# Twelve 256-column projections of a two-layer trunk by seven quarter products instead of eight, the weight sums on GpSimd

## The reference, cut to what matters

```
for l in range(2):
    h = rmsnorm(x, attn_norm[l])                 # 256 tokens x 1024
    proj = h @ w_in[l]                           # 1024 x 3088: pa, pb, pc, pd side by side
    oa = rmsnorm(window_attention(rope(q, k), v, sinks))       # from pa: P11, P12
    ob = rmsnorm(gla_chunked(q, k, v, log_a)) * silu(g)        # from pb: P7, P8, P9/P10
    oc = rmsnorm(stick_breaking_attention(q, k, v))            # from pc: P4, P5, P6
    od = rwkv7_time_mix(pd, ...)                               # from pd: P0, P1, P2, P3
    x = x + concat(oa, ob, oc, od) @ w_out[l]
    h = rmsnorm(x, ffn_norm[l])
    x = x + (dense_swiglu(h) if l == 0 else top2_of_8_experts(h))
return rmsnorm(x, final_norm)
```

## Time and profile before

| | |
|---|---|
| Time, median of 3 runs | 960.59 us (960.5 to 961.04) |
| The profiled execution | 963.35 us, its span 961.4 us |
| PE busy | 945.6 us (98% of the span) |
| DVE, ACT, POOL busy | 379.5, 182.1, 146.7 us (39%, 19%, 15%) |
| Mean granted TensorE clock | 0.992 of full speed |
| Moved | 223.18 MB, mean 232 GB/s |

### The profile page before, as it was taken

How to read it: one execution, slowest core, us unless ns; L and a number is a source line. 1 busy time by engine, 2 the same in 40 slices (tenths; PEclk the granted TensorE clock), 3 DMA queues, 4 the chain that set the end, 5 groups by cost and what they waited for, 6 DMA issues and landing times.

```text
span 961.4 us, 28523 instructions
## 1 busy us (share of the span) xinstructions
PE 945.6 (98%) x12808; PEld 752.7 (78%) x12808; DVE 379.5 (39%) x811; ACT 182.1 (19%) x400; POOL 146.7 (15%) x164
## 2 busy tenths in 40 slices
PE   9999999999999999999999999999999999999996
PEld 8887875699999644788787659878878696969692
DVE  3415676476666555341566433122121213030204
ACT  3345241211111000224514121010000001010102
POOL 2000532033333421000063100000000000000000
PEclk9999999999999999999999999999999999999998
DMA  9843201545555545344310696999999999999931
GB/s 318 268 132 132 89 2 45 161 137 171 170 169 173 212 177 174 127 134 134 130 62 3 211 410 245 400 348 403 396 399 399 401 388 412 387 413 386 400 123 44
DMA packets 90114, 223.18 MB, mean 232 GB/s; under 512 B 6080, under 2 KB 53952, under 8 KB 89920
## 3 DMA queue, kind: packets, MB, share of 16 engines
q1 hardware_dynamic: 86528, 212.29, 59.6%
q0 software_dynamic: 1680, 5.90, 2.5%
q10 hardware_dynamic: 1840, 4.00, 1.3%
HBM read 215.89 MB, written 6.29 MB: 231 GB/s over the span
## 4 chain that ended last, share of the span: by engine, by line
PE 97%; ACT 2%; DVE 1%; issue 1%; POOL 0%; DVEq 0%; POOLq 0%; ACTq 0%
PE bank L629 94%; PE bank L640 1%; PE bank L1265 1%; ACT arena L1554 0%; PE bank L1008 0%; ACT hT L1409 0%; ACT arena L1551 0%; ACT arena L1414 0%; PE bank L976 0%; DVE arena L2036 0%; PE bank L779 0%; DVE hT L1855 0%; PE bank L803 0%; DVE arena L1804 0%; ACT arena L1527 0%
## 5 line engine op out<-in xcount | busy, mean ns | idle before, releaser
L629 PE MATMUL bank<-arena 128*64 128x96 f32 (+6 forms) x8592 | 504.9, 276 | 3.6 <-issue 1.4
L629 PEld LDWEIGHTS bank<-arena 128*64 128x64 f32 (+4 forms) x8592 | 381.3, 137 | 125.8 <-issue 103.9
L629 PE MATMUL bank<-hT,arena 128*64 128x128 f32 (+2 forms) x1548 | 164.5, 307 | 1.5 <-ACT hT L1409 0.9
L629 PEld LDWEIGHTS bank<-hT,arena 128*64 128x64 f32 (+2 forms) x1548 | 145.6, 152 | 16.4 <-issue 4.4
L1804 DVE TENSOR_TENSOR arena<-arena 128x512 f32<-128x512 f32 (+3 forms) x139 | 125.0, 913 | 51.2 <-ACT arena L1414 26.3
L629 PE MATMUL bank<-arena,hT 128*128 128x256 f32 (+3 forms) x556 | 135.1, 404 | 0.2
L629 PEld LDWEIGHTS bank<-arena,hT 128*128 128x128 f32 (+2 forms) x556 | 88.9, 181 | 36.4 <-issue 26.5
L1804 DVE TENSOR_TENSOR arena<-arena,bank 128x128 f32<-128x128 f32 (+3 forms) x135 | 48.9, 391 | 131.9 <-ACT arena L1617 104.5
L629 PE MATMUL bank<-tok,arena 128*64 128x128 f32 x1408 | 81.0, 273 | 0.0
L629 PEld LDWEIGHTS bank<-tok,arena 128*64 128x64 f32 x1408 | 78.2, 137 | 0.0
L1414 ACT COPY arena<-bank 128x512 f32<-128x512 f32 (+2 forms) x63 | 31.0, 496 | 173.3 <-PE bank L629 171.1
(11 more groups left out here) (207 smaller groups left out, 537.0 us busy)
## 6 DMA issues: line engine op xcount, KB each, us to landing
arena<-in_moe_w SPq DMA_DIRECT2D x128, 704.0 KB, 11.1
arena<-in_moe_w SPq DMA_DIRECT2D x40, 1024.0 KB, 8.8
arena<-in_ffn_w SPq DMA_DIRECT2D x33, 1024.0 KB, 5.6
arena<-in_w_in SPq DMA_DIRECT2D x22, 1024.0 KB, 5.3
arena<-in_w_out SPq DMA_DIRECT2D x8, 1024.0 KB, 4.9
arena<-in_moe_w SPq DMA_DIRECT2D x8, 512.0 KB, 12.7
arena<-in_w_in SPq DMA_DIRECT2D x2, 1088.0 KB, 5.8
consts<-in_consts SPq DMA_DIRECT2D x1, 1330.5 KB, 7.6
```

Of the source, the lines that this page charges most:

```text
L629: return nc.tensor.matmul(o, lhsT, rhs, start=start, stop=stop, skip_group_check=True)
```

## The change

Twelve projections go by quarters: P2, P3, P5, P6, P7 in layer 0 and P0, P1, P2, P3, P5, P6, P7 in layer 1. For each of them:

- POOL sums the piece (`projection_piece_sums`): s1 = w21 + w22, s2 = s1 - w11, s4 = w12 - s2, then s3 = w11 - w21, four instructions of 128 x 512, into one of two sets of buffers. Set 0 is a new tensor `extra`, set 1 lies over `normed` and `b_att`. The sums of a projection wait until the projection that used the set before is full.
- PE runs seven products of 4 x 2 matmuls in place of 16 matmuls of 128 x 256: two from the weights themselves, one with s4, then s2, s1, s3 and w22 with the sums of `hT`. The results lie in two banks, `P..a` and `P..b`.
- ACT copies one quarter (128 x 128) into `first_piece` in place of the whole result (`first_quarter`); DVE combines the rest in five instructions (`quarters_out`).

DVE takes the sums of `hT` in both layers ahead of the mixing (`feature_sums`). The memset of `b_att` moves from the start of the kernel to behind the full P7 of each layer. In layer 1 POOL sums P0 before its two `row_powers`, and P1 after the rows are scaled (`h_ready`) and dn0 is evacuated. P0 and P1 of layer 0, and P4, P8 to P12 of both layers, stay as they were. The start has 35 short products in place of 36, and the first 29 of the products of `between_blocks` are issued as two of 64 columns each in place of one of 128.

```
+QUARTERED = [f"P{i}" for i in (2, 3, 5, 6, 7)], [f"P{i}" for i in (0, 1, 2, 3, 5, 6, 7)]
+QUARTERED_ORDER = [(l, name) for l in range(DEPTH) for name in QUARTERED[l]]
...
+_SETS = ((0, 1), (6, 7))
+PROJECTION_BANKS = [[] for _ in range(DEPTH)]
+for _l in range(DEPTH):
+    for _i in range(7):
+        if f"P{_i}" in QUARTERED[_l]:
+            PROJECTION_BANKS[_l] += [(f"P{_i}a", _SETS[_i % 2][0]), (f"P{_i}b", _SETS[_i % 2][1])]
+        else:
+            PROJECTION_BANKS[_l].append((f"P{_i}", _i % 4))
...
+        extra = sb("extra", [P, 3 * 512 + 2 * P])
...
+        first_piece = [extra[:, 1536 + P * b:1536 + P * b + P] for b in range(2)]
+        sum_parts = [[extra[:, 512 * i:512 * i + 512] for i in range(3)],
+                     [part("normed")[:, 0:512], part("normed")[:, 512:1024], part("b_att")]]
...
             def between_blocks(n):
-                idle_products(n, banks[2], ident[:, 0:HALF], consts[:, 0:P])
+                for _ in range(n):
+                    halved[0] += 1
+                    if halved[0] <= HALVED:
+                        idle_products(2, banks[2], ident[:, 0:HALF], consts[:, 0:HALF])
+                    else:
+                        idle_products(1, banks[2], ident[:, 0:HALF], consts[:, 0:P])
...
+            def quarter_product(o, weights, features, tokens, start=False):
+                for k in range(KC // 2):
+                    a, b = (features, weights) if tokens else (weights, features)
+                    last = mm_halves(o, a[:, k, :], b[:, k, :], start=(start and k == 0), stop=(k == KC // 2 - 1))
+                return last
+            def quarters_first(name, l, features=None, tokens=False):
+                wait_piece(pe, projection_piece(name, l))
+                w11, w12, _, _ = projection_quarters(name, l)
+                wait_open(pe, f"{name}a", l)
+                a = bank(f"{name}a", l)
+                for i in (0, 1):
+                    if features:
+                        wait_evacuated(pe, features[i], l)
+                quarter_product(a[:, 0:P], w11, hT[:, 0:KC // 2, 0:P], tokens, start=True)
+                for i in (2, 3):
+                    if features:
+                        wait_evacuated(pe, features[i], l)
+                quarter_product(a[:, P:2 * P], w12, hT[:, KC // 2:, 0:P], tokens)
+            def quarters_third(name, l, tokens=False):
+                k, _, _, _, s4 = projection_sums(name, l)
+                pe.wait_ge(sem("piece_summed"), k + 1)
+                wait_open(pe, f"{name}b", l)
+                at = 3 * P if tokens else 2 * P
+                quarter_product(bank(f"{name}b", l)[:, at:at + P], s4, hT[:, KC // 2:, P:SEQ], tokens, start=True)
+            def quarters_rest(name, l, tokens=False):
+                _, s1, s2, s3, _ = projection_sums(name, l)
+                _, _, _, w22 = projection_quarters(name, l)
+                a, b = bank(f"{name}a", l), bank(f"{name}b", l)
+                pe.wait_ge(sem("h_summed"), 4 * H_SUMS[l, 0] + 4)
+                fills(quarter_product(a[:, 2 * P:3 * P], s2, h_sums[:, 1], tokens), f"{name}a", l)
+                at = P if tokens else 0
+                quarter_product(b[:, at:at + P], s1, h_sums[:, 0], tokens)
+                pe.wait_ge(sem("piece_subtracted"), QUARTERED_ORDER.index((l, name)) + 1)
+                quarter_product(b[:, P - at:2 * P - at], s3, h_sums[:, 2], tokens)
+                at = 2 * P if tokens else 3 * P
+                fills(quarter_product(b[:, at:at + P], w22, h_sums[:, 3], tokens), f"{name}b", l)
+            def project_quarters(name, l, tokens=False):
+                quarters_first(name, l, tokens=tokens)
+                quarters_third(name, l, tokens)
+                quarters_rest(name, l, tokens)
...
-                project_features("P0", l, n0, both, ("T0", "T1", "T2", "T3"))
-                project_features("P1", l, n0 + 1, both)
-                project_features("P2", l, n0 + 2, both)
+                if "P0" in QUARTERED[l]:
+                    quarters_first("P0", l, ("T0", "T1", "T2", "T3"))
+                    quarters_third("P0", l)
+                    quarters_first("P1", l)
+                    quarters_rest("P0", l)
+                    quarters_third("P1", l)
+                    quarters_rest("P1", l)
+                else:
+                    project_features("P0", l, n0, both, ("T0", "T1", "T2", "T3"))
+                    project_features("P1", l, n0 + 1, both)
+                project_quarters("P2", l)
...
-                project_features("P3", l, n0 + 3, both)
+                project_quarters("P3", l)
...
-                project_features("P5", l, n0 + 5, both)
-                project_tokens("P6", l, n0 + 6, GW)
+                project_quarters("P5", l)
+                project_quarters("P6", l, tokens=True)
...
-                project_features("P7", l, n0 + 7, both)
+                project_quarters("P7", l)
...
+            def first_quarter(name, l):
+                wait_full(act, f"{name}a", l)
+                if set_before(name, l):
+                    before, other = set_before(name, l)
+                    wait_evacuated(act, f"{other}b", before)
+                nc.scalar.copy(first_piece[set_of(name, l)], bank(f"{name}a", l)[:, 0:P]).then_inc(sem("quarter_copied"), 1)
...
-                evacuate("P5", l, c_k, both(bank("P5", l)[:, :]))
-                evacuate("P6", l, c_v, both(bank("P6", l)[:, :]))
+                first_quarter("P5", l)
+                first_quarter("P6", l)
...
+            def projection_piece_sums(name, l):
+                k, s1, s2, s3, s4 = projection_sums(name, l)
+                wait_piece(pool, projection_piece(name, l))
+                if set_before(name, l):
+                    before, other = set_before(name, l)
+                    wait_full(pool, f"{other}b", before)
+                w11, w12, w21, w22 = projection_quarters(name, l)
+                link(g.tensor_tensor(s1, w21, w22, ALU.add))
+                link(g.tensor_tensor(s2, s1, w11, ALU.subtract))
+                g.tensor_tensor(s4, w12, s2, ALU.subtract).then_inc(sem("piece_summed"), 1)
+                g.tensor_tensor(s3, w11, w21, ALU.subtract).then_inc(sem("piece_subtracted"), 1)
...
-            g.memset(b_att[:, :, :, :], 0.0)
...
                 if l:
+                    projection_piece_sums("P0", l)
                     row_powers()
+                    pool.wait_ge(sem("h_ready"), 2 * NT * (norm_index(l, 0) + 1))
+                    wait_evacuated(pool, "dn0", l - 1)
+                for name in QUARTERED[l][l:]:
+                    projection_piece_sums(name, l)
+                wait_full(pool, "P7b", l)
+                g.memset(b_att[:, :, :, :], 0.0).then_inc(sem("att_cleared"), 1)
                 for c in range(NT):
...
+            def quarters_out(name, l, dst, step=P, tokens=False):
+                k = QUARTERED_ORDER.index((l, name))
+                a, b, first = bank(f"{name}a", l), bank(f"{name}b", l), first_piece[set_of(name, l)]
+                def pair_of(ap, width):
+                    return ap.rearrange("p (i t) -> p i t", i=2)[:, :, 0:width]
+                middle = pair_of(dst[:, P:P + 2 * step], P)
+                dve.wait_ge(sem("quarter_copied"), k + 1)
+                tt(dst[:, 0:P], first, a[:, P:2 * P], ALU.add)
+                frees(tt(first, first, a[:, 2 * P:3 * P], ALU.add), f"{name}a", l)
+                wait_evacuated(dve, f"{name}a", l)
+                wait_full(dve, f"{name}b", l)
+                link(tt(middle, pair_of(b[:, 0:2 * P], P), over(first, 2), ALU.add))
+                u3, p5 = (middle[:, 0, :], b[:, P:2 * P]) if tokens else (middle[:, 1, :], b[:, 0:P])
+                link(tt(dst[:, 2 * P + step:3 * P + step], u3, p5, ALU.add))
+                frees(tt(middle, middle, pair_of(b[:, 2 * P:4 * P], P), ALU.add), f"{name}b", l)
+                wait_evacuated(dve, f"{name}b", l)
...
                     dve.wait_ge(sem("cleared"), 1)
+                feature_sums(("T0", "T1", "T2", "T3"), l, H_SUMS[l, 0])
                 mix_tokens("P0", l, 6)
...
+                quarters_out("P5", l, region_f[:, 0:512])
+                quarters_out("P6", l, region_f[:, 512:1024], tokens=True)
...
+                quarters_out("P7", l, region_m[:, 2568:3080])
...
-            def feature_sums(l):
+            def feature_sums(names, l, use):
...
-WARM_UP_SHORT = 36
+WARM_UP_SHORT = 35
+HALVED = 29
```

73 lines of the change are left out of this document (52 added, 21 removed), and 4 rows, old and new, of the table uses.

## The result

| | before | after |
|---|---|---|
| Median of 12 runs each | 961.25 us (960.42 to 967.3) | 954.95 us (953.96 to 958.7) |
| Profiled execution, its span | 963.35, 961.4 us | 956.03, 954.2 us |
| Mean granted clock of it | 0.992 | 0.996 |

The ratio is 0.9929, with a 95% interval of 0.9913 to 0.9946: faster by 6.3 us, where the forecast was 8.2. The time lies in the range. The difference is 0.7%, and the interval lies clear of 1.

A forecast was written before the change was run, and what follows sets the result against it. PE was taken to bound the kernel: exchange -10.17, joints +0.4, P0's later start +0.2 and the wait for hT's sums +1.4 make -8.2 us, from the median 960.59 to 952.4, range 948.5 to 956.6.

The forecast's parts named there:

- The price of 6.11 us for a quartered projection: On PE, seven quarter products take 6.11 us, read from one half piece of the dense feed-forward.
- The wait for the sums of hT: Layer 1, P0: PE waits 1.4 us for DVE's sums, slowed by POOL's sums of P1; bounds 0 and 2.1.
- POOL and DVE's combining: POOL's forty-eight sums and DVE's five combining instructions per projection stay covered by PE's work: cost 0.
- the tight covers at P2: POOL's sums ready ahead of PE: 2 us in layer 0, tightest 0.5 to 2 at contended price; cost 0.
- POOL's start of P2: Layer 1: POOL starts P2's sums when P0 is full, about 404 us.
- its own signs of being wrong: Wrong if PE's gaps in the mixers grow by over 3 us or a quartered projection takes over 6.4.
- the third rival: POOL's sums become the bound and the kernel gets slower, 965.5 us at the contended price; chance 0.05.
- The joints: On PE, where runs of unlike shape meet: some eight more meetings at 0.05 us, +0.4, between 0 and 0.9.
- the exchange: On PE, twelve whole projections (83.49 us) replaced by quartered ones (73.32) give back 10.17 us.
- The products without use: Products of 64 columns in place of 128 keep PE as long: cost 0.
- The clock: Granted clock: no change, ends -4.1 and +3.2 us; as a rival, chance 0.13 better, 0.10 worse.
- the chance of "slower": That the changed kernel measures slower than the one before: 0.05.

The follow-up runs named there:

- best_all: late_p1 together with halves_all, the latter with 15 halved products without use in place of 29: 953.85 us.
- late_p1: The changed kernel, but in layer 1 POOL starts its sums of P1 only after DVE's four sums of hT: 955.27 us.
- twice: The changed kernel, but POOL takes s1, s2 and s4 of each quartered projection twice, seven sums per projection: 972.52 us.
- plain_idle: The changed kernel with the products without use as before the change, 36 short ones and none halved: 1024.53 us.
- after_again: The changed kernel run again without any edit: 955.65 us, ratio 0.9933.
- held: The changed kernel, but SP holds expert 1's weight rows until PE has used six of the first expert's eight: 951.78 us in a single run.
- before_14: The kernel before the change, nothing quartered, with its first 14 128-column products without use issued as two of 64: 1010.93 us.
- best_proj: late_p1 and halves together: 954.34 us.
- halves: The changed kernel, with the 128-output-partition products of projections that still go whole issued as two of 64: 953.79 us.
- halves_all: halves, with the low-rank products LW, LA and G and the product KN also issued as halves: 1000.66 us.

## Why the prediction came out as it did

**Right, by its own steps.** The direction, the bound, and that PE alone counts. The price of 6.11 us for a quartered projection: in best_all, where nothing of another shape stands beside it, P7 takes 448.06 - 441.95 = 6.11. The wait for the sums of hT was at its place, ended by what was named, and its cause is shown by late_p1. POOL and DVE's combining cost nothing, and the tight covers at P2 were real (`twice`). POOL's start of P2, expected about 404, was 401.79, as that is less 2.48. By its own signs of being wrong it stands: no quartered projection took over 6.4 us, and the gaps in the mixers grew by under 1. One slip is in the third rival, which adds 1.8 us for the other additions where its own terms make 2.0; nothing hangs on it.

**The joints were mis-sized**: "eight more such meetings; I take 0.05 each, +0.4, between 0 and 0.9". In layer 0 the exchange was to give 5 x 0.85 = 4.23 us (34.78 less 5 x 6.11), and gave 3.17; in layer 1 5.94, and gave 4.04 with a wait of 0.87. So the joints cost 1.06 + 1.03 = 2.1 us, beyond the bound. The mistake was the row they were taken from: P3 against P7 in the earlier trace rows prices a meeting with LW's small tiles, and what the change makes is a meeting of 128*64 with 128*128 tiles, which no row there has. P3 and P7 took 0.15 more than 6.11, LA 0.11 more than in the earlier trace rows (420.35 - 419.38 = 0.97 against 0.86), P8 0.10 more. Nor is it a cost of the new form alone, since P7 takes 6.11 once its neighbours have its shape. Giving all the same shape brought back 0.74 in layer 0 and, from 1.46 with late_p1's 0.89 taken off, 0.57 in layer 1: 1.3 of the 2.1. The rest is not assigned.

**The wait was 0.87, not 1.4**, a size only. Against the steps, moved by the 2.48 us that layer 1 starts earlier: DVE began its sums at 393.22 for 393.5, lost 1.93 us in the overlap (0.87 and 1.06 of the two sums that it struck) for 2.0 to 2.3, and was ready at 397.9 for 398.3; PE wanted them at 397.05 for 396.9, since P0 started later.

**The products without use** were costed at nothing and took +0.30 between P10 of layer 0 and layer 1's first transposition (a block of eight, now sixteen halves, takes 2.08 us for 1.96, one of four 1.15 for 1.09); `plain_idle`, without them, takes 305.85 us there, the kernel before 305.84. The +0.39 ahead of the first transposition stays unassigned: with 36 short products as before, `plain_idle` comes to it at 9.27, later than the 9.06 of the changed kernel, and equal starts spread over a microsecond.

**The clock was right as "no change", and wrong as a rival.** I gave it 0.23 as an effect of the change. The same kernel shows one fall in one profile and none in another, so it is a property of the execution. It made 2.9 us of the difference of the two profiled spans, and hid 1.9 us that the first expert lost.

**What no step of the prediction had** is the experts' code. The queue of instruction loads was on the page, 54 packets, and the later passes, 44.91 us each without a gap, say that the loop's code stays loaded. The diff's last lines moved the loop's place by 56 records of products and as many of weight loads, and the prediction read them as nothing but time on PE. With the term known, the chance of "slower" hangs on one count: whether the change and its filler keep the loop's start where it was. It did: the stalls of the first pass lie 624 records (496 and 128) behind the same product after, and 623 before. That this came out is no merit of the prediction: without the filler the same twelve projections measured 1024.53 us, and neither the forecast nor a rival had a reason for that. In this part the hit was luck.

**The sum again**, in the profiled pair: -10.17 + 2.1 (joints) + 0.39 (start, unassigned) + 0.30 (filler) + 0.33 (P0's start, of which 0.2 was foreseen) + 0.87 = -6.2 at 469 us; then -2.9 from the clock and +1.9 from the first pass, -7.2. In the medians it is -6.3, close to the mixers alone, as if the 1.9 were not there. An estimate of the reason: from P10 of layer 1 to the experts an execution without falls takes 114.04 us (after_again and held), and behind the first pass every profile with eight packets in the loop takes 337.0 to 337.1. The kernel before spans 958.6 us in the median of its 20 runs at 0.998. With its P10 at 469.17 that leaves 958.6 - 337.0 - 114.04 - 469.17 = 38.4 us for its first pass, where its profiled execution, which came to the experts late through two falls, took 36.8. So in executions without falls both kernels lose about the same there. `before_14`, which starts the experts 2.8 us earlier than the kernel before, took 38.2. How much of this is the earlier start stays open: `best_proj` starts 4.3 us ahead of `halves` and takes only 0.2 longer (37.72 and 37.49).

## What to carry to other kernels

Before costing an edit to an engine's program, look whether a hot loop follows it: count its instructions, and the page's packets of code per pass; where a loop just fits, any edit ahead of it can move it over an edge that is worth more than the edit, and a few instructions without use can move it back. Price a new shape of matmul with its neighbours' shape in mind, some 0.1 to 0.15 us for each change between 128*128 and 128*64 tiles here, and take two executions' traces before a clock stretch is counted for or against a change. A transfer that is issued as early as it can be is not free: look what else must load in that stretch.

## What the runs showed of the hardware

- A loop of 848 matmul records and as many weight loads stays with PE when its code lies in seven 16 KB blocks: 44.9 us a pass, eight packets of code once. When it lies in eight, nine packets are loaded in every pass, and a pass takes 50 to 56 us (halves_all, plain_idle, before_14), clock falls included.
- Code loads come late beside weights that move at 400 GB/s: stalls of up to 1.8 us a block in the first pass of the versions that keep the loop's place, none where the same stretch moved 33 GB/s (`held`).
- Two matmuls of 64 output partitions cost no more than one of 128: P8 and P9 took 13.98 us in best_all and in the kernel before.
- DVE's `scalar_tensor_tensor` with both inputs in SBUF took 2.80 us for two of 128 x 256 beside POOL's sums (at 403.72), 0.88 in the kernel before.
